# Decoder step on eight cores: sample units given a full step each in layer 0, and the fourth head of each band unit scaled on VectorE

## What is computed

```python
def cross_attention(qm, mk, mv):            # 4 heads of 128, 256 memory tokens
    s = einsum('nqhd,nmhd->nhqm', q, mk) * 128 ** -0.5
    p = softmax(s)
    return einsum('nhqm,nmhd->nqhd', p, mv)

def band_attention(q, kk, vv, sinks, key_valid):   # 24 heads of 64, 4 kv heads
    s = where(band & key_valid, einsum('nkgqd,njkd->nkgqj', q, kk) * 64 ** -0.5, -inf)
    m = maximum(max(s), sink)
    e = exp(s - m)
    p = e / (sum(e) + exp(sink - m))
    return einsum('nkgqj,njkd->nqkgd', p, vv)
```

## Time and profile before

| | |
|---|---|
| time, median of 3 runs | 2915.32 us (2914.01 to 2915.5) |
| profiled execution, its own time | 2913.25 us |
| its span, slowest core (core 2) | 2911.7 us |
| even cores | 2909.0 to 2911.7 us |
| odd cores | 2867.1 to 2871.7 us |
| busy on core 2: TensorE / VectorE / ScalarE / POOL | 2829.2 / 952.7 / 510.9 / 396.0 us |

### The profile page before, as it was taken

The page is one execution under the profiler, slowest core; times in us unless marked ns, Lnnn a source line. Parts: engine busy times, 40 slices in busy tenths (PEclk is TensorE's granted clock), DMA queues, the critical chain, the costliest instruction groups (busy, mean ns, idle before and its releaser), DMA issues.

```text
span 2911.7 us, 51081 instructions; the slowest of 8 cores (2867.1 to 2911.7 us)
## 1 busy us (share of the span) xinstructions
PE 2829.2 (97%) x18868; PEld 1780.1 (61%) x18868; DVE 952.7 (33%) x2004; ACT 510.9 (18%) x1410; POOL 396.0 (14%) x700
## 2 busy tenths in 40 slices
PE   6999999999999999999999899999999999999997
PEld 3665666666666666666656545566666666666664
DVE  2425436331302113131162568544131221312116
ACT  3213203100010000000133666220000000000013
POOL 0013111000000100001002667100000010000100
PEclk9999999999999999999999999999999999999999
DMA  8485447344352642525324412734317254252513
GB/s 191 90 131 84 74 69 123 73 81 89 83 100 51 122 75 51 90 41 102 51 44 82 81 31 46 122 59 87 73 21 122 48 93 70 42 101 44 102 30 124
DMA packets 79768, 232.59 MB, mean 80 GB/s; under 512 B 10208, under 2 KB 25184, under 8 KB 79488
## 3 DMA queue, kind: packets, MB, share of 16 engines
q0 software_dynamic: 60912, 204.83, 40.3%
q1 hardware_dynamic: 18608, 24.42, 2.7%
HBM read 424.86 MB, written 11.12 MB: 150 GB/s over the span
## 4 chain that ended last, share of the span: by engine, by line
PE 92%; DVE 2%; issue 2%; ACT 1%; POOL 1%; DMA 1%; SPq 1%; DVEq 0%; ACTq 0%; POOLq 0%
PE bank L430 91%; POOL sb_rc L442 1%; ACT sb_rc L436 1%; DMA sb_rx<-xe 1%; PE bank L433 1%; SPq L453 1%; DVE sb_st L605 0%; DVE bank L601 0%; DVE sb_st L651 0%; DVE sb_rx L439 0%; DVE sb_rc L445 0%; DVE sb_rx L445 0%; DVE sb_rc L439 0%; ACT sb_rn L436 0%; DVE sb_rc L459 0%
## 5 line engine op out<-in xcount | busy, mean ns | idle before, releaser
L430 PE MATMUL bank<-sb_ra,sb_rs 128*128 128x368 bf16 (+2 forms) x4672 | 807.8, 320 | 3.1 <-DVE sb_ra L445 2.0
L430 PE MATMUL bank<-sb_rb,sb_rs 128*128 128x368 bf16 (+3 forms) x4176 | 711.8, 317 | 3.6 <-ACT sb_ra L436 3.1
L430 PEld LDWEIGHTS bank<-sb_ra,sb_rs 128*128 128x128 bf16 x4672 | 453.3, 98 | 267.2 <-issue 20.1
L430 PEld LDWEIGHTS bank<-sb_rb,sb_rs 128*128 128x128 bf16 x4176 | 402.7, 98 | 234.1 <-issue 12.4
L439 DVE TENSOR_TENSOR sb_rx<-sb_rx,bank 128x368 f32<-128x368 f32 (+3 forms) x768 | 406.7, 531 | 416.0 <-PE bank L430 407.3
L436 ACT ACTIVATE sb_rc<-bank 128x368 f32<-128x368 f32 (+7 forms) x346 | 157.6, 456 | 1815.6 <-PE bank L430 1811.8
L430 PE MATMUL bank<-sb_rb,sb_rc 128*128 128x368 bf16 (+3 forms) x2576 | 441.6, 318 | 0.0
L430 PE MATMUL bank<-sb_ra,sb_rc 128*128 128x368 bf16 (+2 forms) x2304 | 403.3, 316 | 0.0
L430 PEld LDWEIGHTS bank<-sb_rb,sb_rc 128*128 128x128 bf16 x2576 | 251.9, 98 | 145.4
L430 PEld LDWEIGHTS bank<-sb_ra,sb_rc 128*128 128x128 bf16 x2304 | 225.4, 98 | 126.4
L439 DVE TENSOR_TENSOR sb_rb<-sb_rc,bank 128x368 bf16<-128x368 f32 (+2 forms) x180 | 91.0, 506 | 591.2 <-PE bank L430 589.6
(11 more groups left out here) (107 smaller groups left out, 1298.0 us busy)
## 6 DMA issues: line engine op xcount, KB each, us to landing
sb_rc<-w_up POOLq DMA_DIRECT2D x43, 512.0 KB, 7.4
sb_rs<-w_down POOLq DMA_DIRECT2D x42, 512.0 KB, 6.2
sb_rs<-w_gate POOLq DMA_DIRECT2D x40, 512.0 KB, 6.9
sb_rs<-conv_w_in POOLq DMA_DIRECT2D x36, 512.0 KB, 6.4
sb_rc<-w_gate POOLq DMA_DIRECT2D x31, 512.0 KB, 6.1
sb_rs<-w_up POOLq DMA_DIRECT2D x28, 512.0 KB, 8.5
sb_rc<-w_down POOLq DMA_DIRECT2D x24, 512.0 KB, 6.8
sb_rs<-w_out_a POOLq DMA_DIRECT2D x32, 320.0 KB, 4.1
```

The source lines that it names most:

```text
L430: P.op("pe", lambda e: e.matmul(out, lhsT=lhsT, rhs=rhs, start=start, stop=stop), r=r, w=w)
```

## The change

Two edits. In layer 0 a sample unit's `share` becomes 1.0 instead of 0.5, so its step takes 25 and 25 ticks instead of 12 and 13; in layer 1 (`l` is 1) it stays 0.5. And in `u_self` the fourth head's scaling goes to VectorE ("dve"), heads one to three stay on POOL.

```diff
             def stat():
                 rcp(d["st"][:, 16:20], d["st"][:, 4:8], d["sr"], d["sr"])
-                scale_p(d, [(hd, 128, 128) for hd in range(4)])
+                scale_p(d, [(hd, 128, 128) for hd in range(4)], ("pool", "pool", "pool", "dve"))
...
             sk_, sv_ = smk[s_ % 2], smv[s_ % 2]
-            d["share"] = 0.5
+            d["share"] = 0.5 if l else 1.0
```

## The result

The changed kernel takes 0.9942 [0.9918, 0.9966] of the time before, some 16.9 us less; two executions took 2898.47 us (the profiled one) and 2897.32 us. I had forecast 2905.8 us and a range from 2899.5 us, so it was faster than forecast and just outside the range. (All comparisons and means leave out executions, or dies, that ran at a lower clock throughout.)

The account below looks back on a forecast made before the run. Even cores bound the time, with TensorE 97% busy; -8.8 us (first edit) and -0.7 us (layer 1) sum to -9.5 us, giving a predicted median of 2905.8 us. Own range 2903 to 2909 us; with A, B and C 2899.5 to 2911.5.

Parts of the forecast that it names:

- What bounds the kernel: Whole kernel: even cores (2911.7 us) set the time; TensorE is 97% busy, so effects go through its idle time and clock.
- First edit, waits: Layer 0's convolution: TensorE's waits for VectorE's copy of transposed probabilities fall from 8.7 to 1.6 us, saving 7.1 us.
- First edit, clock: Layer 0's convolution: the 3.4 us at half clock after a long stall go, saving 1.7 us.
- Second edit, waits: Layer 1's attention: POOL waits fall by 4.3 and 0.6 us, PV waits 4.2 us more for the mask multiply: -0.7 us.
- the step that failed first: Layer 1's attention: 16 of 27 waits for POOL are at a fourth head, 4.3 us in all, and go.
- The step that failed second: Layer 1's attention: three long stalls where POOL starts late stay, 6.5 us, and the half clock behind them too.
- The sum: Even cores: -8.8 us from the first edit and -0.7 us from layer 1 give -9.5 us.
- A: Both edits pay in full, PV never waits longer: -15.1 us, 2900.2 us; chance 0.14.
- B: Layer 0's waits move: 2.8 to 5 us remain, half clock too; sum -5.2 us, 2910.1 us; chance 0.17.
- C: Layer 1: VectorE's lag also delays freeing PSUM banks, layer 1 +3.1 us; sum -5.7 us, 2909.6 us; chance 0.13.
- D: Layer 1: VectorE's piece waits for a running POOL head, 0.97 us more per unit; +8.9 us, 2924.2 us; chance 0.06.

Follow-up runs that it names:

- shifted grids: The changed kernel with its layer-0 feed started 4, 8, 12, 16 or 24 ticks later: 2899.8, 2899.4, 2899.0, 2898.1 and 2900.6 us.
- seven pairs: All heads on POOL against the fourth on VectorE, with the old share, the new share and five later feed starts: VectorE faster by 1.7 to 4.7 us.
- shifted twins: Feed started 4, 8, 12, 16 or 24 ticks later, all heads on POOL (2901.0 to 2905.4 us) or the fourth on VectorE (2898.1 to 2900.6 us).
- first edit alone: The changed kernel with the fourth head's scaling back on POOL: 0.9957 of the time before, 2902.1 us.
- share 0.75: All heads on POOL, sample units' share in layer 0 at 0.75, steps of 18 and 19 ticks: 2904.35 us (one execution).

## Why the prediction was wrong, step by step

- **What bounds the kernel**: right. The even cores stayed the slowest in every kernel.
- **First edit, waits**: right in kind, -7.1 forecast and -8.7 measured. On the kernel's own grid nothing is left of the 1.6 us that I took. That this is partly luck is shown by the shifted grids: 1.7, 1.2, 0, 0.9 and 2.3 us are left on core 2 with shifts of 4, 8, 12, 16 and 24. So 1.6 was a fair forecast over grids. The last PV of layer 0 moved from 341.81 to 363.62 us, as 31 us of added ticks less 10 us of saved time would have it, and comes 13 us before the convolution ends, as forecast.
- **First edit, clock**: right in that no half clock is left; the four even cores had had 4.3 us on average, not only core 2's 3.4. The reading behind it, that a stall of 3 us is followed by one stretch, was too simple: the kernel before has stalls of 3.06 and 2.88 us on every even core, and core 2 has no stretch at the second (281.3 us), core 0 none at the first; only core 4 has both. The convolution is 10.7 us shorter, where I had 8.8. That the edit costs nothing holds: after the load near 1900 us, and in layer 1, nothing moved (400.4 us both).
- **Second edit, waits**: nearly right. POOL -5.6 (forecast -4.9) and mask multiply +2.7 (forecast +4.2), but ScalarE's and the copy's rows rose by 3.5 us on core 2, part of them again at PV, whose idle time rose by 4.5 us in all. The sum is +0.6 against -0.7.
- **Second edit, the step that failed first**: "Sixteen of the 27 waits are at a fourth head, 0.16 to 0.36 us each, 4.3 us in all". This took the list of waits for all of POOL's lateness. The part that left no gap stood in TensorE's busy time, 4.1 to 4.7 us of it on average of the even cores. Of this the stage got back 2.6 us at equal clock; 1.3 us went into the same hidden lateness at PV and 0.3 us into idle time. That this term was missing, and not only small, is shown on seven pairs.
- **The step that failed second**: "The half clock behind them stays too." From before to after it went from 22.2 to 11.9 us a core. By the stage times the gain in layer 1 is 5.3 us, so some 2.7 us are the clock's. The long stalls did stay (1.91 + 0.36 + 0.36 us on core 2), as forecast, but they got half as much half clock: the stall of 2.07 us at 1659 us had 6.8 us of it before, the one of 1.91 us in its place has none on cores 0 and 2 and 3.4 us on cores 4 and 6. The shifted twins show that this is not the edit's own doing: it depends on where the stalls fall, and the kernel before and the first edit alone sat on unlucky grids (22.2 and 21.3 us, against 14.2 on the shifted ones).
- **The sum** on the profiled executions: -9.5, a further -1.9 in layer 0, -1.9 for the stretched transposes less what PV lost (-2.6 instead of -0.7), -2.7 for the clock in layer 1, and +0.9 at the start, which no edit touches: -15.1 us, as measured (-10.7 - 5.3 + 0.9). The terms were split from these same differences, so that they add up is no further test.
- **Rivals**: A gave nearly the right time (2900.2 us) for a wrong reason: PV does wait longer. B did not happen, nor did C's loss. D is refuted: VectorE's piece takes 0.255 us in the median beside POOL pieces of 0.60 us, and the mask multiply comes 0.35 us later, not 0.97. The rule of the Trainium skill ("SBUF — State Buffer", Who interferes with whom), by which a VectorE tensor_scalar in a two-port mode and a POOL instruction block each other for a whole instruction, does not describe these pieces: at 1740.55 and 1740.61 us above they started together and neither was prolonged. Whether the piece ran in such a mode no run here shows, so the rule itself is not tested.

**What stays open**: what decides, for a given stall, between none, 3.4 and 6.8 us or more at half clock. Its place in time matters, and cores of one kernel with the same waits differ; more than that these runs do not tell. Nor is it known why the start differs by 0.9 us.

## What to carry to other kernels

A list of waits is not all of an engine's lateness: where matmuls overlap, look also at the busy time of the group that consumes the late data, and compare it with count times spacing. A one-off change of a few microseconds that goes with a change of the granted clock should be repeated on a few shifted orders before the edit gets the credit; here that took a gain of 4 to 5 us down to about 3. Without the new orders the clock's share would have passed for the edit's. And in an in-order queue, move the copy or the scaling that stands behind somebody else's wait before you divide the work any finer: that gave 7.6 us on the one order tried, more than the second edit.

## What the runs showed of the hardware

- Four transposes in a row take 0.39 us when ready, and 0.42 to 0.70 in the kernel before (core 2, full clock) when an input comes late without a wait in the list; the profile counts nearly all of it as busy.
- With 20.9 and 21.3 us of waits, two cores of one kernel spent 23.9 and 10.2 us at 1.2 GHz. A single stall of 2.8 us in layer 0 (share 0.75, core 0) was followed by none, and of the two stalls of 3.06 and 2.88 us in the kernel before only one went with a stretch on cores 0, 2 and 6, and both on core 4.
- In layer 1's attention a DMA issue holds POOL's queue for 0.53 to 0.59 us, six in a row for 3.18 us, and a scaling behind them starts that much later.
- Added work on VectorE that made TensorE wait 2.8 us more for it lengthened the stage by 1.0 us only, since TensorE's waits for POOL fell by 2.3 us and its stretched transposes by 1.2 us, and 2.5 us less of half clock fell in the stage.
- Beside a running POOL scaling a 128x128 scaling on VectorE took 0.255 us in the median, 41 pieces of 48 overlapping one for more than half of their time.
